# Delta stage of a hybrid DeltaNet and attention layer: each tile's state products, output transposes and next preparation placed between the levels of another tile's inverse

## The reference, cut to what matters

```python
decay = exp(where(tri_incl, gcum[..., :, None] - gcum[..., None, :], -inf))
kb = kc * bc[..., None]
L = where(tri_strict, einsum('bnhid,bnhjd->bnhij', kb, kc) * decay, 0.0)
tinv = triangular_solve(eye + L, eye, left_side=True, lower=True)
w = tinv @ (kb * eg[..., None])
u = tinv @ (vc * bc[..., None])
attn = einsum('bnhid,bnhjd->bnhij', qc, kc) * decay
def step(S, xs):
    vnew = u_ - w_ @ S
    o = qg_ @ S + attn_ @ vnew
    S = S * gl_[..., None, None] + swapaxes(kd_, -1, -2) @ vnew
```

## Time and profile before

| | us |
|---|---|
| median of 3 runs | 2204.53 (2202.8 to 2205.09) |
| the profiled execution | 2205.74 |
| span of its trace, first to last instruction | 2204.1 |
| delta stage in the trace, first transpose to last gated output | 1473.61 to 1885.12 |
| first tile's levels begin | 1492.02 |
| sample tile's levels begin | 1843.55 |

### The profile page before, as it was taken

The page is one execution under the profiler, slowest core; times in us unless marked ns, Lnnn a source line. Parts: engine busy times, 40 slices in busy tenths (PEclk is TensorE's granted clock), DMA queues, the critical chain, the costliest instruction groups (busy, mean ns, idle before and its releaser), DMA issues. The chain is left out here.

```text
span 2204.1 us, 32063 instructions
## 1 busy us (share of the span) xinstructions
PE 1993.9 (90%) x12297; PEld 1824.0 (83%) x12297; DVE 942.2 (43%) x2003; ACT 607.5 (28%) x1006; POOL 204.1 (9%) x256
## 2 busy tenths in 40 slices
PE   6899999999999999959856889978889888799999
PEld 2699999999999999947745678767878887699977
DVE  1555444100100100056434656557777777514342
ACT  2433332111111222133223554333323332202110
POOL 0022111000000000000003321210100010000000
PEclk9899999999999999979976999999999999899999
DMA  8222233222232222231011212041113212623232
GB/s 314 69 107 85 92 111 111 92 100 92 92 111 81 98 104 76 76 104 44 24 48 48 68 44 59 20 134 39 58 58 106 66 58 67 217 85 127 68 119 76
DMA packets 153707, 195.40 MB, mean 89 GB/s; under 512 B 9153, under 2 KB 124910, under 8 KB 153628
## 3 DMA queue, kind: packets, MB, share of 16 engines
q1 hardware_dynamic: 142300, 151.85, 20.5%
q0 software_dynamic: 10064, 38.13, 5.1%
q10 hardware_dynamic: 1264, 4.39, 0.5%
HBM read 134.15 MB, written 60.19 MB: 88 GB/s over the span
## 5 line engine op out<-in xcount | busy, mean ns | idle before, releaser
L1938 PE MATMUL PS<-HH,WL 128*128 128x352 f32 (+1 forms) x1752 | 379.8, 325 | 5.3 <-DVE mod L2048 5.3
L1938 PE MATMUL PS<-HH,WH 128*128 128x352 f32 (+1 forms) x1752 | 378.3, 323 | 0.0
L1938 PE MATMUL PS<-HL,WH 128*128 128x352 f32 (+1 forms) x1752 | 378.0, 324 | 0.0
L2044 DVE TENSOR_TENSOR WL<-Wraw,WH 128x2048 fp32r<-128x2048 f32 x37 | 84.8, 2293 | 523.0 <-ACT WH L1881 523.0
L1938 PEld LDWEIGHTS PS<-HH,WL 128*128 128x128 f32 (+1 forms) x1752 | 298.7, 189 | 5.6 <-issue 5.3
L1938 PEld LDWEIGHTS PS<-HH,WH 128*128 128x128 f32 (+1 forms) x1752 | 301.1, 188 | 0.3
L1938 PEld LDWEIGHTS PS<-HL,WH 128*128 128x128 f32 (+1 forms) x1752 | 297.8, 188 | 0.2
L1909 ACT ACTIVATE R<-PS 128x1056 f32<-128x1056 f32 x48 | 50.6, 1053 | 409.1 <-PE PS L1938 409.1
L1450 PE MATMUL PS<-WT,QL 128*128 128x128 f32 x832 | 114.3, 295 | 20.6 <-DVE QL L1686 19.3
L1450 PEld LDWEIGHTS PS<-WT,QL 128*128 128x128 f32 x832 | 105.6, 206 | 29.1 <-DVE QL L1686 29.1
L1686 DVE COPY_PREDICATED QL<-lev,PS 128x512 f32<-128x512 int32 x122 | 86.8, 733 | 57.3 <-PE PS L1468 51.8
(11 more groups left out here) (294 smaller groups left out, 3080.9 us busy)
## 6 DMA issues: line engine op xcount, KB each, us to landing
scratch_proj<-R SPq DMA_DIRECT2D x72, 576.0 KB, 2.8
Wraw<-in_w_in POOLq DMA_DIRECT2D x36, 1024.0 KB, 5.4
QKV<-scratch_proj SPq DMA_DIRECT2D x27, 512.0 KB, 6.2
Wraw<-in_w_ada SPq DMA_DIRECT2D x12, 1024.0 KB, 5.5
fr<-scratch_u SPq DMA_DIRECT2D x16, 528.0 KB, 5.3
gr<-scratch_proj SPq DMA_DIRECT2D x16, 528.0 KB, 3.5
qraw<-scratch_proj SPq DMA_DIRECT2D x9, 768.0 KB, 5.0
zb<-scratch_proj SPq DMA_DIRECT2D x18, 256.0 KB, 3.1
```

Of the source, the lines that this page charges most:

```text
L1938: last = pe.matmul(PS[0:m, psum + b, 0:TB], w[:, s, k, c * P:c * P + m], h[:, k, b * TB:(b + 1) * TB], start=(k == 0 and first), stop=(k = ...
L2044: dve.tensor_tensor(WL[:, s], Wraw[:, s], WH[:, s].bitcast(F32), ALU.subtract).then_inc(s_wlo, 1)
```

## The change

The delta stage is written out for nine iterations n = 0 to 8, without a loop. In iteration n the levels of tile n run, and between them PE gets fillers: the state products of tile n - 1, the preparation of tile n + 1, and the output transposes of tile n - 3. Level l has two places for fillers, one between the two transposes and the two products, and one behind the products; the table `FILL` says what stands in each. What is left of tile 8 and of the last outputs follows behind iteration 8.

With it go these edits:

- The decay difference moves from DVE (subtract and min) to ACT as a Relu with a scalar for each head (eight instructions a tile), in level 2, and the exponential in level 3.
- ACT sums the squares of k while squaring them, with the accumulator, one head at a time, and copies k to `Kt` with a scale for each head; so `ZD` is gone, and with it one scaling of 512 columns for each group on DVE. Vn, the output scaling and the output's squares (with accumulator) are done by ACT too, one head at a time. DVE keeps the sums of the q squares.
- The inverse root is now split over levels 2 (`dve_norm_begin`), 3 (`dve_norm_steps`) and 4 (`dve_norm_end`). The output's normalisation is joined with it, two tiles late.
- In levels 5 and 6 the predicated copy gives way to plain copies of the blocks alone (four of 32 partitions, two of 64 for both groups together).
- `QKV` and `Kt` have three slots, `AT`, `O2` and `UA` two; the copy of a tile's scalars to `tv` by POOL is gone, and S is cleared by POOL. Semaphores are one for each kind of step, and some are merged. The next stage is unchanged but for an address.

```diff
-                if not last and l in (0, 1, 3):
-                    pe_prep(pe, t + 1, 1 - slot, {0: "k", 1: "q", 3: "v"}[l], prev=not first)
...
+    FILL = {(0, 0): (("ks", 0),), (0, 1): (("ks", 1), ("k", 0)),
+            (1, 0): (("on", 0), ("k", 1)), (1, 1): (("on", 1), ("q", 0)),
+            (2, 0): (("y", 0),), (2, 1): (("y", 1), ("q", 1)),
+            (3, 0): (("st", 0), ("qs", 0)), (3, 1): (("st", 1), ("qs", 1)),
+            (4, 0): (("av", 0), ("v", 0)), (4, 1): (("av", 1), ("v", 1)),
+            (5, 0): (("kk", 0),), (5, 1): (("kk", 1),),
+            (6, 0): (("qk", 0),), (6, 1): (("qk", 1),)}
...
+    def pe_fill(pe, n, l, half):
+        of_next = {"k": pe_k, "q": pe_q, "v": pe_v, "kk": pe_kk, "qk": pe_qk}
+        of_state = {"ks": pe_ks, "qs": pe_qs, "y": pe_solve, "st": pe_state, "av": pe_attended}
+        for name, g in FILL[l, half]:
+            if name in of_next and n + 1 <= NT:
+                of_next[name](pe, n + 1, g)
+            if name in of_state and n >= 1:
+                of_state[name](pe, n - 1, g)
+            if name == "on" and n >= 3:
+                pe_out(pe, n - 3, g)
...
+    def pe_v(pe, p, g, b=2):
+        if p >= 2:
+            pe.wait_ge(d_o1, nth(p - 2, g))
+        elif p:
+            pe.wait_ge(d_qq, nth(p, g))
+        pe_turn_four(pe, bank(g, b), lambda h: QKV[:, p % 3, 2 * H + 4 * g + h], d_vt)
...
+    def pe_qs(pe, t, g):
+        st = 1 if t == NT else 0
+        if t + 2 <= NT:
+            pe.wait_ge(d_qq, nth(t + 2, g))
+        else:
+            pe.wait_ge(d_at, nth(NT, g))
+        pe_four(pe, bank(g, 2), lambda h: QKV[:, t % 3, 4 * g + h], lambda h: S[:, st, 4 * g + h], d_qs)
...
+    def pe_attended(pe, t, g, b=1):
+        if b == 1:
+            pe.wait_ge(d_s, nth(t, g))
+        else:
+            pe.wait_ge(d_z, nth(t, g))
+        pe_four(pe, bank(g, b), lambda h: hs(AT[:, g, t % 2], h), lambda h: hs(Z[:, g], h), d_av)
...
+        for n in range(NT + 1):
+            for l in range(NL7):
+                if l < levels(n):
+                    for g in range(2):
+                        pe_level_turn(pe, n, l, g)
+                pe_fill(pe, n, l, 0)
+                if l < levels(n):
+                    for g in range(2):
+                        pe_level_product(pe, n, l, g)
+                pe_fill(pe, n, l, 1)
...
+    def act_decays_of(act, p, part):
+        if part == "exp":
+            act.drain()
+        for g in range(2):
+            if part == "relu":
+                if g == 0:
+                    act.wait_ge(s_gb[p % 2], 16 * (p // 2 + 1))
+                if p:
+                    act.wait_ge(d_em, nth(p - 1, g))
+                for h in range(4):
+                    act.activation(hs(E[:, g], h), GB[:, p % 2, (4 * g + h) * P:(4 * g + h + 1) * P], ACT.Relu,
+                                   bias=tvs[:, p, 0, 4 * g + h:4 * g + h + 1], scale=-1.0)
...
+    def act_k(act, p, g):
+        act.wait_ge(d_k, nth(p, g))
+        for h in range(4):
+            act.activation(hs(sq[:, g], h), hs(bank(g, 2), h), ACT.Square, accum_out=ksum[:, g, h:h + 1])
+        for h in range(4):
+            x = act.activation(hs(Kt[:, g, p % 3], h), hs(bank(g, 2), h), ACT.Copy, scale=tvs[:, p, 3, 4 * g + h:4 * g + h + 1])
+        x.then_inc(d_kt, 1)
...
+                if l == 2 and more:
+                    act_decays_of(act, n + 1, "relu")
+                    act_q(act, n + 1, 0)
+                if l == 3:
+                    if more:
+                        act_q(act, n + 1, 1)
+                    if n >= 1:
+                        act_state_output(act, n - 1, 0)
+                    if more:
+                        act_decays_of(act, n + 1, "exp")
+                    if n >= 1:
+                        act_state_output(act, n - 1, 1)
+                if l == 4:
+                    if more:
+                        act_v(act, n + 1, 0)
+                    if n >= 2:
+                        act_normalise(act, n - 2, 0)
...
+    def pool_masked(pool, p):
+        for g in range(2):
+            pool.wait_ge(d_e, nth(p, g))
+            if p:
+                pool.wait_ge(d_nl, nth(p - 1, g))
+                pool.wait_ge(d_at, nth(p - 1, g))
+            for out, m in ((Es, K_STR), (Em, K_INC)):
+                x = pool.tensor_tensor(heads(out[:, g]), heads(E[:, g]), cst[:, m:m + P].unsqueeze(1).to_broadcast([P, 4, P]), ALU.mult)
+            x.then_inc(d_em, 1)
...
+    def dve_norm_end(dve, p, w):
+        if p is not None:
+            v = vec[:, p % 4]
+            beta = tvs[:, p, 5].rearrange("p (g h) -> p g h", g=2)
+            dve.tensor_tensor(v[:, 1], krs, krs, ALU.mult)
+            dve.tensor_tensor(v[:, 0], kss, krs, ALU.mult)
+        if w is not None:
+            dve.tensor_scalar(ost[:, w % 2], ors, 1.0, None, ALU.mult)
+        if p is not None:
+            dve.drain()
+            dve.tensor_tensor(v[:, 1], v[:, 1], beta, ALU.mult)
+            dve.drain()
+            dve.tensor_scalar(v[:, 2], v[:, 1], -1.0, None, ALU.mult)
+        dve.drain().then_inc(s_nrm, 1)
...
+        if l < NL7 - 2:
+            x = dve.copy_predicated(heads(QL[:, g, l]), level_mask(l), heads(bank(g, 0)))
+        else:
+            s = LEVELS[l]
+            for c in range(0, P, 2 * s):
+                x = dve.tensor_copy(heads(QL[:, g, l])[c + s:c + 2 * s, :, c:c + s], heads(bank(g, 0))[c + s:c + 2 * s, :, c:c + s])
...
+        for n in range(NT + 1):
+            p = n + 1 if n + 1 <= NT else None
+            t = n - 1 if n >= 1 else None
+            w = n - 2 if n >= 2 else None
+            for l in range(NL7):
+                if l < levels(n):
                     for g in range(2):
+                        dve_level(dve, n, l, g)
+                if n == 0 and l == 0:
+                    identities(range(2, NL7))
+                if l == 0:
                     for g in range(2):
+                        dve_masked_qk(dve, n, g)
+                    if t is not None:
+                        dve_right_side(dve, t, 0)
+                if l == 1:
+                    if t is not None:
+                        dve_right_side(dve, t, 1)
+                    if n >= 3:
+                        for g in range(2):
+                            dve_u(dve, n - 3, g)
+                if l == 2:
+                    if t is not None:
+                        dve_z(dve, t, 0)
+                    dve_norm_begin(dve, p, w)
+                if l == 3:
+                    if t is not None:
+                        dve_z(dve, t, 1)
+                        dve_state(dve, t, 0)
+                    dve_norm_steps(dve)
                 if l == 4:
+                    dve_norm_end(dve, p, w)
+                    if t is not None:
+                        dve_state(dve, t, 1)
+                        dve_output(dve, t, 0)
+                if l == levels(n) - 1 and n == NT:
+                    for g in range(2):
+                        dve_inverse(dve, n, g)
+                if l == 5:
+                    if t is not None:
+                        dve_output(dve, t, 1)
+                    if p is not None:
+                        dve_q_sums(dve, p)
+                if l == 6 and n < NT:
+                    for g in range(2):
+                        dve_strict(dve, p, g)
+                        dve_inverse(dve, n, g)
```

More of the change, by code:

```diff
@@ L1037, in build @@
-    s_ac = {n: [sem(f"delta_act_{n}_{g}") for g in range(2)] for n in ("prep", "main", "out")}
-    s_dv = {n: [sem(f"delta_dve_{n}_{g}") for g in range(2)] for n in ("prep", "main", "out")}
-    s_em = [sem(f"masked_decays_ready_{g}") for g in range(2)]
-    SKIPPED = tuple(f"{a}{l}" for l in range(NLS, NL7) for a in "tvq") + tuple(f"x{l}" for l in range(NLS - 1, NL7 - 1))
-    s_seen = sem("level_transpose_seen")
-    def after(eng, sems, steps, g, t, step):
-        made = [x for x in steps if x not in SKIPPED] if isinstance(t, int) and t == NT else steps
-        eng.wait_ge(sems[g], len(steps) * t + made.index(step) + 1)
@@ L1405, in sp_delta @@
         sp_store_u(sp, NT)
[L1406 to L1407 removed]
+        sp.wait_ge(s_so, 48)
         sp.wait_ge(s_ua, 32 * (NT + 1))
[L1411 to L1423 removed]
@@ new lines, in pe_turn_four, with pe_k, pe_q @@
+    def pe_turn_four(pe, out, src, done):
+        for h in range(4):
+            last = pe.transpose(hs(out, h), src(h), ident)
+        last.then_inc(done, 1)
+    def pe_k(pe, p, g):
+        pe.wait_ge(s_in[p % 3], 48 * (p // 3 + 1))
+        if p:
+            pe.wait_ge(d_at, nth(p - 1, g))
+        pe_turn_four(pe, bank(g, 2), lambda h: QKV[:, p % 3, H + 4 * g + h], d_k)
+    def pe_q(pe, p, g, b=2):
+        pe.wait_ge(d_kt, nth(p, g))
+        pe_turn_four(pe, bank(g, b), lambda h: QKV[:, p % 3, 4 * g + h], d_q)
```

736 lines of the change are left out of this document (370 added, 366 removed).

## The result

The changed kernel takes **2174.32 us** (median of 4 executions, 2173.4 to 2175.32), the kernel before, measured beside it, 2204.81: a ratio of 0.9863, 95% interval 0.9851 to 0.9875. Forecast: 2174. Measured once more at the end of the study it took 2175.71 (ratio 0.9866, 0.9851 to 0.9881). The profiled execution took 2174.75 us, its span is 2173.1.

A forecast was written before the change was run, and what follows sets the result against it. PE was taken to bound the kernel, leading but waiting some 9.5 us a tile. Iterations 33 us less, head 4 less, tail 7 more: 30 off the profiled 2205.7, 2175.7, with the median 1.2 lower: 2174 us; range 2142 to 2192.

The forecast's parts named there:

- passes: PE's work in a full tile: 312 passes at 0.112 us each, 34.9 us.
- small waits: PE waits for ACT's q squares (0.45 and 0.6 us) and the strict matrix (0.3): together 1.3 us a tile.
- the wait for the state: Level 4: PE's second attended product waits 3.3 us because POOL's masks hold three dependent norm steps on DVE.
- the low clock: Slow PE passes behind the level 4 wait for the state, priced at 1.6 us a tile.
- Iterations 1 and 2: Iterations without output transposes, 8 passes fewer than a full one: 40.2 us each.
- The head: Before the first level: POOL's first mask product shortens from 4.53 to 1.26 us, levels begin 4 us earlier.
- The tail: From the sample tile's levels to the last gated output: 48.5 us against 41.6, 7 us more.
- The rest: Everything outside head, iterations and tail, including QKV's and w_o's loads: no change.
- rival 1: Level 4: the norm is not held, PE waits 0.4 instead of 3.3 us, clock stays up: 2142 us, chance 0.18.
- rival 2: Level 4: the norm is held but the clock stays up, 11 us less: 2163 us, chance 0.20.
- rival 3: More PE waits, ACT's queue delaying copies of the levels or v, 2 us a tile: 2188 us, chance 0.17.
- rival 4: PE stays long at low clock behind the level 4 wait: 2255 us, slower from 8.6 us a tile; chance 0.08.

The follow-up runs named there:

- norm early with q first: Changed kernel with DVE's norm_end moved to the end of level 3 and ACT's squares of q put ahead of the Relus: 2132.45 us.
- masks late: Changed kernel with POOL's four masks of a tile waiting until DVE has written S of the second head group: 2143.63 us.
- PE kept busy: Changed kernel with PE repeating 24 transposes of v of the next tile during the level 4 wait for S: 2162.02 us.
- the first two experiments: Changed kernel with, separately, DVE's norm_end moved to the end of level 3 (2139.43 us) and POOL's masks waiting for DVE's S (2143.63 us).
- variant with q first: Changed kernel with ACT's squares of q of the next tile put ahead of its four Relus: 2168.59 us, repeated at 2169.28.

## Why the prediction was right, step by step

**A full iteration.** Forecast 41.1 = 34.9 + 1.3 + 3.3 + 1.6; measured 40.76. The runs give each term: passes 34.62 (norm early with q first), small waits 35.83 - 34.62 = 1.21, the wait for the state 39.11 - 35.83 = 3.28, the low clock behind it 40.76 - 39.11 = 1.65. All four sizes held, and the causes of the two large ones are shown, not only argued: that the masks hold DVE by masks late, that idle brings the low clock by PE kept busy. The order in time held as well. From the transposes of level 4 in the iteration of 1641.09 (T = 1662.71) the masks run from T + 0.78 to T + 5.75 (forecast 0.8 to 5.8), the state is there at T + 7.1 (7.2) and the attended product starts at T + 7.16 (7.3). No row before had shown an instruction with two inputs on eight columns beside POOL; L1759 and L1764 are such, and both were held (1.25 and 1.08 us), so all three steps were, as the forecast took it, and not two. The small waits are right by offsetting errors: they stood where they were looked for, but at 0.41 and 0.28 of idle instead of 0.45 and 0.6, the third, 0.3 for the strict matrix, did not appear, and what made up for it is that a wait costs more than its idle, which the forecast did not count.

**Iterations 1 and 2** were put at 40.2 each and took 38.6 and 40.2. **The low clock** was charged to every iteration and came in five of seven. This is the term that was mis-sized, by 2 x 1.65 = 3.3 us, and with the 0.3 a tile above it makes the eight iterations 313.2 instead of 318.4. The rows before could have told: behind the wait of level 5 the clock had stayed up in one tile of five. How often it falls is not fixed, either: in the repeat of the changed kernel it fell in six of the seven (iteration 1 too, 40.26 us), and the eight iterations took 316.1, only 2.3 less than forecast.

**The head** is the step that failed. Forecast -4, measured -1.3. POOL's first mask is short now, as said (4.53 before, 1.27 now), but the price of the lock, applied to level 4 and to iteration 0, was left out of the head: norm_end of tile 0 stands beside the masks there too, and PE waits 6.5 us for Vn. From DVE's timeline in the changed kernel:

```profile
1480.74 1.29 DVE L1758 TENSOR_TENSOR vec<-RS 128x8 f32<-128x8 f32 x1
1481.95 0.15 DVE L1759 TENSOR_TENSOR vec<-RS 128x8 f32<-128x8 f32 x1
1482.18 1.08 DVE L1764 TENSOR_TENSOR vec<-vec,decay 128x8 f32<-128x8 f32 x1
1483.33 1.15 DVE L1766 TENSOR_SCALAR vec<-vec 128x8 f32<-128x8 f32 x1
```

With the masks moved away the head falls to 14.3 us, 4.1 under the kernel before, though iteration 0 takes a part of that back. The price was not new in this head: in the kernel before, L1599 is a step of the same chain of tile 0, held there for 1.15 us, so a part of it was in the 18.4 already. How the rest of the 2.7 us divides is not shown.

**The tail** was put at 48.5 (its parts add up to 48.6) and took 47.9. **The rest** was put at 0 and shows +2.3 in the profile, -1.4 ahead and +3.7 behind, but the profiles spread by 5 us and more in each of these stretches, and the repeat of the same kernel has 2.9 us less behind. So 5.2 us more gained in the iterations and 0.6 in the tail stood against 2.7 less in the head and 2.3 lost in the rest; that the sum met the median to 0.3 us is partly luck.

**The rivals.** That the norm is not held (rival 1, 2142) is what the first two experiments made true by edits, 2139 and 2144: its price was right, its condition did not hold. That the clock stays up (rival 2, 2163) is what PE kept busy made true, at 2162; of its 12 us only 8 are the clock, since it had fallen in five iterations and not in the seven that I counted. That more waits appear (rival 3) did not come: ACT is busy for 24.8 us of an iteration, not 27.6, and PE never waits for its copies WT in a full iteration. The slower case (rival 4) needed 8.6 us of low clock a tile; the change has 3.4. The variant with q first has 6.8, so the rival was nearer than the 3.4 suggest.

The Trainium skill, "SBUF — State Buffer", section "Who interferes with whom", states the lock between VectorE and GpSimd as held for the whole instruction; the trace agrees, with ends 0.02 to 0.03 us apart on instructions of eight columns. By that section's list of kinds L1766, with one SBUF input, is held only if it runs in a two-port mode; here it was held in all nine cases, at 1.15 us. The runs themselves show only that DVE's instruction ends with POOL's, not what the two engines share.

## What to carry to other kernels

Once fillers cover an engine's waits, what is left are places where a short dependent chain on DVE lies beside POOL's long operations: n small steps cost up to n of POOL's, so put the chain ahead of them, or let POOL wait for it. Price a wait by what it does to the distance between starts, not by its idle alone, and the low clock behind it as a term of its own; and try an edit on the clock with the clock held up, since a gain at one wait can be taken back at the next. A mechanism found in the loop has to be looked for in the head as well.

## What the runs showed of the hardware that was not expected

Fewer pauses made the clock worse: with the two waits of 0.41 and 0.28 us gone, and the one behind them hardly longer (3.07 to 3.31 instead of 3.00), the clock was low for 6.8 us instead of 3.4 and a late iteration's mean fell from 0.96 to 0.92, in both profiles of that kernel. Why is open. Repeating passes whose results are not needed made the kernel 12 us faster (2162.0 against 2174.3), of which 8, in iterations 1 to 7, are the clock. And DVE's instructions with an operand in PSUM and its reductions, on 512 columns, ran beside the masks at their own speed, while those on eight columns in SBUF took seven times theirs: it is not their size that decides.
